# A two-layer hybrid decoder trunk on one core: other orders in the mixer stage, per-head scalar normalisation, and level masks on VectorE

## The reference, cut to what matters

```python
D_MODEL, SEQ, DEPTH = 2048, 256, 2
for l in range(DEPTH):
    h = rms_norm(x, attn_norm[l])
    hq, hf, hi, hg, mq, mkv, mkr, rw = split_cols(h @ w_in[l], IN_SIZES)
    o_hg = hgrn2_mixer(hq, hf, hi, hg, ...)             # gated linear recurrence, 4 heads of 128
    o_mla = mla_mixer(mq, mkv, mkr, cos, sin, ...)      # latent attention, 8 heads, rotary key
    o_rw, v_first = rwkv7_mixer(rw, ...)                # RWKV-7 time mixing, 8 heads of 64
    x = x + jnp.concatenate([o_hg, o_mla, o_rw], -1) @ w_o[l]
    gate, up = jnp.split(rms_norm(x, ffn_norm[l]) @ w_gate_up[l], 2, -1)
    x = x + (silu(gate) * up) @ w_down[l]

def causal_block_attention(...):        # inside mla_mixer, per head
    s = (q_nope . k_nope + q_rope . k_rope) * scale, causal mask
    p = softmax(s);  out = p @ v

def rwkv7_mixer(...):                   # per head and token t
    sa = state @ (-kk_t)
    state = state * w_t + outer(sa, kk_t * a_t) + outer(v_t, k_t)
    y_t = state @ r_t
    out = (group_norm(y) + bonus) * g,  bonus = sum(r * k * r_k) * v
```

## Time and profile before

| | |
|---|---|
| median of three runs | 2364.59 us (2363.1 to 2364.89) |
| the profiled execution's own time | 2363.51 us |
| its span | 2361.7 us |
| PE busy | 2329.8 us, 99% of the span |
| DVE busy | 1331.0 us, 56% |
| ACT busy | 1090.3 us, 46% |
| GpSimd busy | 60.6 us, 3% |
| granted TensorE clock | 1.0 over the whole span |

### The profile page before, as it was taken

One profiled execution on the slowest core, in us unless ns is written; L12 is line 12 of the kernel. 1 busy time (PEld: TensorE's weight loads), 2 busy tenths in 40 slices (PEclk: granted clock), 3 DMA queues, 4 the chain that ended last, 5 costly groups with the idle time before them and its releaser, 6 DMA issues.

```text
span 2361.7 us, 34240 instructions
## 1 busy us (share of the span) xinstructions
PE 2329.8 (99%) x13929; PEld 1931.9 (82%) x13929; DVE 1331.0 (56%) x1402; ACT 1090.3 (46%) x1336; POOL 60.6 (3%) x60
## 2 busy tenths in 40 slices
PE   8999999999999999999999999999999999999999
PEld 7888688888888888888888886888888888888887
DVE  5686676544545445455556857665454554454444
ACT  6554644444443344444445546455444433444443
POOL 0000210000000000000000002100000000000000
PEclk9999999999999999999999999999999999999999
DMA  7453304555555555555554532045555555555553
GB/s 297 165 185 134 115 18 164 193 181 194 191 182 196 192 190 189 195 183 191 186 189 152 196 113 102 21 165 190 183 192 195 179 195 196 192 185 193 189 187 141
DMA packets 59523, 407.11 MB, mean 172 GB/s; under 512 B 6608, under 2 KB 6704, under 8 KB 13200
## 3 DMA queue, kind: packets, MB, share of 16 engines
q1 hardware_dynamic: 58720, 401.66, 47.4%
q0 software_dynamic: 688, 3.78, 0.5%
HBM read 403.32 MB, written 2.10 MB: 172 GB/s over the span
## 4 chain that ended last, share of the span: by engine, by line
PE 94%; DVE 5%; issue 1%; ACT 0%; DMA 0%; DVEq 0%; SPq 0%; ACTq 0%
PE psum L1447 28%; PE psum L1449 28%; PE psum L1448 28%; PE psum L1641 2%; PE psum L1889 1%; PE psum L1736 1%; PE psum L1976 1%; PE psum L1542 1%; PE psum L1481 1%; DVE arena L1192 1%; DVE arena L1262 0%; DVE small L1176 0%; DVE arena L1173 0%; PE psum L1717 0%; DVE arena L1283 0%
## 5 line engine op out<-in xcount | busy, mean ns | idle before, releaser
L875 DVE TENSOR_TENSOR w_lo<-raw,w_hi 128x1024 fp32r<-128x1024 f32 (+2 forms) x752 | 901.5, 1205 | 848.7 <-ACT w_hi L450 841.8
L450 ACT ACTIVATE w_hi<-raw 128x1024 fp32r<-128x1024 f32 (+2 forms) x752 | 781.9, 1044 | 1082.6 <-PE psum L1449 1081.0
L1447 PE MATMUL psum<-w_hi,hT_hi 128*128 128x512 f32 (+2 forms) x2128 | 821.6, 386 | 3.1 <-DVE w_lo L875 3.1
L1449 PE MATMUL psum<-w_hi,hT_lo 128*128 128x512 f32 (+2 forms) x2128 | 816.4, 384 | 0.0
L1448 PE MATMUL psum<-w_lo,hT_hi 128*128 128x512 f32 (+2 forms) x2128 | 816.3, 384 | 0.0
L1447 PEld LDWEIGHTS psum<-w_hi,hT_hi 128*128 128x128 f32 x2128 | 399.8, 188 | 81.7 <-DVE w_lo L875 2.4
L1449 PEld LDWEIGHTS psum<-w_hi,hT_lo 128*128 128x128 f32 x2128 | 399.7, 188 | 78.3
L1448 PEld LDWEIGHTS psum<-w_lo,hT_hi 128*128 128x128 f32 x2128 | 399.9, 188 | 76.5
L1447 PE MATMUL psum<-w_hi,act_hi 128*128 128x512 f32 x872 | 340.4, 390 | 0.0
L1449 PE MATMUL psum<-w_hi,act_lo 128*128 128x512 f32 x872 | 339.4, 389 | 0.0
L1448 PE MATMUL psum<-w_lo,act_hi 128*128 128x512 f32 x872 | 339.3, 389 | 0.0
(11 more groups left out here) (317 smaller groups left out, 1206.9 us busy)
## 6 DMA issues: line engine op xcount, KB each, us to landing
raw<-stream_dram SPq DMA_DIRECT2D x360, 1024.0 KB, 4.8
raw<-stream_dram SPq DMA_DIRECT2D x16, 512.0 KB, 3.5
raw<-stream_dram SPq DMA_DIRECT2D x8, 768.0 KB, 4.2
raw<-stream_dram SPq DMA_DIRECT2D x8, 640.0 KB, 3.7
x<-x_in_dram SPq DMA_DIRECT2D x4, 512.0 KB, 9.2
lor<-lora_dram POOLq DMA_DIRECT2D x2, 832.0 KB, 10.6
con<-consts_dram POOLq DMA_DIRECT2D x1, 1648.0 KB, 12.1
out_dram<-x SPq DMA_DIRECT2D x3, 512.0 KB, 7.4
```

What stands on the lines that cost most here:

```text
L450: nc.scalar.activation(w_hi[:, q % HALF_RING, 0:2 * w], raw[:, j % 4, hf * 2 * w:(hf + 1) * 2 * w], ACT.Copy).then_inc(hi_done, 1)
L875: tt(w_lo[:, q % HALF_RING, 0:2 * w], raw[:, j % 4, hf * 2 * w:(hf + 1) * 2 * w], w_hi[:, q % HALF_RING, 0:2 * w].bitcast(F32), SUB).then_ ...
L1447: mm(o, a_hi, w_hi[:, r, cols], start=(k == 0), stop=False)
L1449: last = mm(o, a_lo, w_hi[:, r, cols], start=False, stop=(k == n_k - 1))
```

## The change

On PE, `up(5)` goes behind the bonus matmuls and `stack(rw_v)`; in layer 0 the stack waits for the shifted values (`rw_shifted`) and no longer for `rw_v_ready`; `product` of `rw_kk` and `rw_a` waits for the bonus product (`rw_bonus_done`); both `r_turn` go ahead of `stack(rw_a)`; `level_x(0)` waits for `rw_m_ready` too. On ACT, `q_out(1)` goes ahead of `up_out(5)`, and `gt_out(2)` ahead of `probs_out(0)`. On DVE, `q_norm()` goes ahead of `rw_a * rw_kk`, the three products with decays follow one another, `k_sums(0)` goes behind the third, and `k_norm(0)` and the bonus behind `rw_k * rw_e_b`; the inverse starts from PSUM directly; the five masks move from GpSimd to DVE, the first behind the start of the inverse, the others in front of the update of a level; `product(1)` moves behind `k_norm(1)`; `probs(p)` multiplies each head by a per-partition scalar.

```diff
@@ gpsimd
-                pool.wait_ge(S("rw_m_ready"), 4 * l + 1)
-                for k in range(len(RW_LEVELS)):
-                    if k:
-                        pool.wait_ge(S("rw_gt_mm"), 10 * l + 2 * k)
-                    tt(rw_level, mab, lev_lo[:, k, :].unsqueeze(1).broadcast_to([P, JC, RC]), ALU.mult).then_inc(
-                        S("rw_level_ready"), 1)
@@ scalar
+                q_out(1)
                 up_out(5)
-                q_out(1)
...
+                gt_out(2)
                 probs_out(0)
                 probs_out(1)
-                gt_out(2)
@@ vector, probs(p)
-                    for off, cols, n in parts:
-                        z = scores[:, h2, cols]
-                        u(tt(z, z, along(small[:, 64 + off + 2 * p:66 + off + 2 * p], n), MUL))
+                    for h in range(2 * p, 2 * p + 2):
+                        for off, cols, n in parts:
+                            z = scores[:, h, cols]
+                            u(ts(z, z, small[:, 64 + off + h:65 + off + h], None, MUL))
@@ vector, the decay part
-                dve.sem_inc(S("rw_v_ready"), 1)
+                    dve.sem_inc(S("rw_v_ready"), 1)
+                q_norm()
                 v(tt(rw_a, rw_a, rw_kk, MUL))
-                q_norm()
                 dve.wait_ge(S("rw_exp"), 3 * l + 1)
                 v(tt(rw_r, rw_r, rw_e_r, MUL))
-                k_sums(0)
                 dve.wait_ge(S("rw_exp"), 3 * l + 2)
                 v(tt(rw_kk, rw_kk, rw_e_kk, MUL))
+                dve.wait_ge(S("rw_exp"), 3 * ev)
+                v(tt(rw_a, rw_a, rw_e_b, MUL))
+                k_sums(0)
+                vs(tt(rw_k, rw_k, rw_e_b, MUL), "rw_ab_done", ev)
                 k_norm(0)
                 dve.wait_ge(S("rw_bonus_mm"), ev)
-                v(tt(rw_bonus.rearrange(flat), bank(2, 2), rw_v.rearrange(flat), MUL))
-                dve.wait_ge(S("rw_exp"), 3 * ev)
-                vs(tt(rw_a, rw_a, rw_e_b, MUL), "rw_b_done", ev)
-                vs(tt(rw_k, rw_k, rw_e_b, MUL), "rw_ab_done", ev)
+                vs(tt(rw_bonus.rearrange(flat), bank(2, 2), rw_v.rearrange(flat), MUL), "rw_bonus_done", ev)
                 k_sums(1)
+                ... (md, three lines, moved here from behind k_norm(1))
@@ vector, level(k)
+                    if not last:
+                        dve.wait_ge(S("rw_gt_mm"), 10 * l + 2 * k + 2)
+                        vs(tt(rw_level, mab, over(lev_lo[:, k + 1, :], JC, RC), MUL), "rw_level_ready", 5 * l + k + 2)
@@ vector, start of the inverse
-                product(1, mab, 2, "strict_lo")
-                v(tt(inv, mab, over(C("pair_lo"), JC, RC), MUL))
+                dve.wait_ge(S("rw_m_mm"), 4 * l + 1)
+                v(tt(inv, bank(2, 2).rearrange("p (n t) -> p n t", n=JC), over(C("pair_lo"), JC, RC), MUL))
                 vs(stt(inv, inv, -1.0, over(idst, JC, RC), MUL, ADD), "rw_x", 10 * l + 1)
                 vs(turn_blocks(inv_t, inv), "rw_xt", 12 * l + 1)
...
+                dve.wait_ge(S("mla_rope_done"), ev)
+                v(tt(rw_level, bank(2, 2).rearrange("p (n t) -> p n t", n=JC), over(lev_lo[:, 0, :], JC, RC), MUL))
+                dve.sem_inc(S("rw_level_ready"), 1)
                 k_norm(1)
+                product(1, mab, 2, "strict_lo")
                 score_max(0)
                 level(0)
@@ tensor
+                        if k == 0:
+                            pe.wait_ge(S("rw_m_ready"), 4 * l + 1)      # in level_x
...
                 if l == 0:
-                    pe.wait_ge(S("rw_v_ready"), ev)
+                    pe.wait_ge(S("rw_shifted"), 4 * l + 3)
                     stack(rw_v, 0)
-                up(5)
...                                             # bonus matmuls
                 if l:
-                    pe.wait_ge(S("rw_v_ready"), ev)
+                    pe.wait_ge(S("rw_v_ready"), l)
                     stack(rw_v, 0)
+                up(5)
                 up(6)
                 up(7)
                 k_turn(0)
-                pe.wait_ge(S("rw_b_done"), ev)
+                pe.wait_ge(S("rw_bonus_done"), ev)
                 product(rw_kk, rw_a, 2)
+                r_turn(range(4))
+                r_turn([4])
                 pe.wait_ge(S("rw_stacked"), 3 * l + 1)
                 stack(rw_a, 0)
-                r_turn(range(4))
-                r_turn([4])
                 attend(0)
```

More of the change, by code:

```diff
@@ L1238, in _ @@
                     v(tt(rw_v, v_first[:, :, :], rw_v, SUB))
-                dve.sem_inc(S("rw_v_ready"), 1)
+                    dve.sem_inc(S("rw_v_ready"), 1)
+                q_norm()
                 v(tt(rw_a, rw_a, rw_kk, MUL))
-                q_norm()
                 dve.wait_ge(S("rw_exp"), 3 * l + 1)
                 v(tt(rw_r, rw_r, rw_e_r, MUL))
-                k_sums(0)
                 dve.wait_ge(S("rw_exp"), 3 * l + 2)
                 v(tt(rw_kk, rw_kk, rw_e_kk, MUL))
+                dve.wait_ge(S("rw_exp"), 3 * ev)
+                v(tt(rw_a, rw_a, rw_e_b, MUL))
+                k_sums(0)
+                vs(tt(rw_k, rw_k, rw_e_b, MUL), "rw_ab_done", ev)
                 k_norm(0)
                 dve.wait_ge(S("rw_bonus_mm"), ev)
-                v(tt(rw_bonus.rearrange(flat), bank(2, 2), rw_v.rearrange(flat), MUL))
-                dve.wait_ge(S("rw_exp"), 3 * ev)
-                vs(tt(rw_a, rw_a, rw_e_b, MUL), "rw_b_done", ev)
-                vs(tt(rw_k, rw_k, rw_e_b, MUL), "rw_ab_done", ev)
+                vs(tt(rw_bonus.rearrange(flat), bank(2, 2), rw_v.rearrange(flat), MUL), "rw_bonus_done", ev)
                 k_sums(1)
+                dve.wait_ge(S("rw_half_decay"), ev)
+                hd = srw[:, 48:64].rearrange("p (j c) -> p j c", j=4)
+                md = srw[:, 64:80].rearrange("p (j c) -> p j c", j=4)
+                v(tt(md[:, :, 0:3], hd[:, :, 0:3], hd[:, :, 1:4], MUL))
                 def product(k, dst, b0, mask):
```

## The result

The changed kernel takes 2371.81 us in the median of seven runs (2370.7 to 2372.1), the kernel before 2363.63 us beside it (2362.8 to 2364.9). The ratio is 1.0034, 95% interval [1.0024, 1.0043]. The forecast was 2366.1 us with a range that ended at 2369.3. By the prediction's own measure of 0.2% that is slower, to which it gave 10%. The profiled execution took 2370.7 us, 7.2 us more than that of before, and was the fastest of the seven.

A forecast was written before the change was run, and what follows sets the result against it. PE, busy 99%, bounds the kernel, with DVE behind most of its gaps. Layer 0 +0.6 - 1.5 + 1.0 = +0.1 us, layer 1 +2.4 - 1.5 + 1.0 = +1.9 us, on 2364.0: 2366.1 us, range 2361.3 to 2369.3.

The forecast's parts named there:

- Part 1 and 2: PE's order in front and DVE's order up to `product`: inverse +0.15 us in layer 0, +1.97 us in layer 1.
- PE's wait of 2.4 to 3 us: Sign: PE waits some 2.4 to 3 us ahead of `k_turn(0)`, for DVE's `k_norm(0)`.
- Part 3: Inverse up to `level_g(2)`: DVE's sum +0.45 us, so `level_g(2)` starts +0.6 us (layer 0) and +2.4 us (layer 1).
- the gap ahead of `level_g(2)`: Sign: PE's gap ahead of `level_g(2)` grows; no size given.
- GpSimd's meetings with DVE: 0.95 us per DVE product of two SBUF operands meeting GpSimd; 4.6 us in layer 1's decay part; line 1283 saves 2.03.
- The 1.0 us for line 1180: Inverse: DVE's two line 1180 instructions no longer meet GpSimd's masks, -1.0 us in all.
- scalar division: `probs(0)` and `probs(1)` on DVE: four scalar multiplications take 1.01 us against 1.02 us for two products, saving 0 us.
- Part 4: From `level_g(2)` to `mix(0)`: `gt_out(2)` earlier and `probs(2)` not held by a mask, -1.5 us in each layer.
- Part 5: Fourth mask on DVE ahead of `level(3)`: PE waits 1.0 us in `level_g(4)`, bounds 0.8 to 1.3.
- A: Rival: GpSimd contention does not come, DVE has 4.6 us less in each layer; 2359.8 us, faster; chance 7%.
- B: Rival: late loss larger, layer 0 behaves as layer 1, `probs` and fourth mask dearer; 2369.6 us, slower; chance 11%.
- C: Rival: PE's gaps in front count in full, slack at the fourth mask; 2363.5 us, no change; chance 22%.

The follow-up runs named there:

- fill: Changed kernel plus 14 unneeded identity transposes on PE ahead of `k_turn(0)` and 12 ahead of `level_g(2)`: 2366.98 us, 1.0013 of before.
- poolmasks: Changed kernel with DVE's decay part in the order of before and masks 1, 2 and 4 on GpSimd again: 2355.95 us, 0.9967 of before.
- olddecay: Changed kernel with DVE's decay part in the order of before, `product` waiting for `rw_a * rw_e_b`: 2366.14 us, 1.0010 of before.
- masks: Kernel before with only the level masks on DVE, the inverse started from PSUM and `product(1)` moved: 2367.37 us, 1.0017 of before.
- late1: Kernel before plus one DVE reduction of 1024 constants ahead of `level(1)` in each layer: 2367.36 us, 1.0017 of before.
- late2: Kernel before plus two DVE reductions of 1024 constants ahead of `level(1)` in each layer: 2368.23 us, 1.0022 of before.
- latehalf: Kernel before plus one DVE reduction of 512 constants ahead of `level(1)` in each layer: 2364.93 us, 1.0008 of before.

## Why the prediction was wrong

The forecast's sum for the work was right, and not by luck: +2.0 us, against 2.3 to 2.9 us in three of the four runs of fill with the clock kept up. Its steps can be read from the trace of fill against that of before, each layer taken from its own start. In layer 0 `level_g(2)` starts +0.8 us (forecast +0.6), `mix(0)` -0.9 (-0.9), the recurrence's first wait ends +0.25 (+0.1); in layer 1 +2.7 (+2.4), +1.0 (+0.9) and +1.9 us (+1.9). In the changed kernel itself those last places come at +2.7 and +4.2 us, 2.4 and 2.3 us behind fill's: two slow stretches in each layer. Step by step, the prediction's number first:

- Part 1 and 2: `k_turn(0)` at 286.2 us, measured 286.38; in layer 1 1462.25, measured 1464.79 less the 2.5 us by which that layer began later. PE's wait of 2.4 to 3 us was forecast and came as 2.83 and 3.22 us. **This is where it failed:** the wait was entered at its own length. The sum held no term for what PE does behind it, though the text named the wait. `product` takes 1.2 to 1.4 us more, and as DVE's inverse waits for it, all of that is on the path.
- Part 3: the gap ahead of `level_g(2)` "grows". I let DVE's sum move the start by +0.6 and +2.4 us and never worked out the gap itself. It is 1.30 + 1.26 = 2.56 us, and the clock falls behind it as well. What DVE's sum should have given in layer 0, 316.7 us, came at 318.20: of the 1.5 us, 1.2 us are the slow `product`.
- GpSimd's meetings with DVE: right in kind and size in the decay part, and at line 1283. The 1.0 us for line 1180 was right for the kernel before, but not a fixed price: in poolmasks the same masks meet next to nothing.
- Part 3, scalar division: 1.01 us for 1.01. Part 4: the order of `gt_out(2)` and the free `probs(2)` went as said; `mix(0)` waits 0.25 instead of 0.1 us. Part 5: 0.68 us for 1.0.
- The rivals: A fell with the first row of 2.17 us. B ended at 2369.6 us by a sum of small lateness, none of which came in that size; the clock was in no case. C did not happen.
- The arithmetic around the sum: 2364.0 + 2.0 is 2366.0 us, not 2366.1, and the stated bounds of -3.5 and +3 us give 2362.6 to 2369.1 us, not 2361.3 to 2369.3. Neither changes the outcome.

Together: 2.3 to 2.9 us of work and waits, and 4.8 us of clock (after less fill). The remaining 0.5 to 1.1 us of the 8.2 us are probably clock too. Seven of fill's eleven runs have a mean clock of 0.999, so fill's median still holds a slow stretch somewhere. The changed kernel shows 0.997 in its profiled execution, with the four slow stretches above, and 0.996 in the six others, which took 0.6 to 1.4 us longer: about one slow stretch more. Only the profiled execution has a trace, so this part is inferred, not shown.

What stays open: what exactly brings the clock down. Behind 2.55 or 2.56 us it fell in olddecay (twice), in the changed kernel (twice), once in masks and once in late1, and held once in masks and once in late1; in late1, fill and masks it also fell in the recurrence, behind waits of 1.07 us and less (in late1 0.49 us and less). Why the low clock lasted twice as long in layer 1 of olddecay and late2 is open too. Of 90 comparable runs of before beside the experiments, 20 show a mean clock of 0.999, the slowest of each set (2364.1 to 2365.4 us).

## What to carry to other kernels

Where PE is busy for 99%, look at the length of each single wait that an edit leaves, not only at their sum: waits up to 1.7 us mostly cost their length here; behind the 18 waits of 2.0 us and more that the mixer stages of all versions show in their profiled executions, the clock fell 16 times, which cost 1.1 to 1.5 us each where no later wait took it up (2.1 us once). Putting work that nobody needs into such a wait paid. Let GpSimd run beside DVE's instructions with an operand in PSUM and its reductions, where it cost DVE next to nothing, rather than giving its work to DVE: three masks a layer on GpSimd instead of DVE were worth 10.2 us, the clock included. A result that PE waits for (`k_norm(0)`) belongs ahead of those that have time.

## What the runs showed of the hardware that was not expected

The granted clock of TensorE falls within a running kernel, on one core, behind a wait of 2.02 us (latehalf, both layers), and the same wait of 2.56 us brings it down in one layer and not in the other (masks). Beside an instruction of GpSimd with both operands in SBUF, DVE's product with one operand in PSUM and its reductions keep their 0.96 and 1.01 us (poolmasks); the GpSimd instruction took 2.46 us there, where two others like it took 2.36 and 2.35 us.
